# Feeding the experts' blocks: a table of tokens and a gather for each block, in place of a scatter through device memory

## The chip, the cores and the metric

One NeuronCore of a Trainium2 chip runs the whole program in one launch. Its engines are TensorE (PE; its weight loads are listed as PEld), VectorE (DVE), ScalarE (ACT), GpSimd (POOL) and SyncE (SP, which here only issues DMAs). They run their own instruction streams and meet at semaphores. The metric is the device time of the launch in microseconds; lower is better.

## The reference, cut to what matters

The reference is one step of a two-layer hybrid decoder on 512 prompt tokens and 32 sample tokens (544 rows of 1024 values, float32). Each layer ends in a mixture of experts:

```python
s = jax.nn.sigmoid((xf @ w_router).astype(f32))          # xf: (544, 1024); 16 experts in 4 groups
... e_idx: the two best experts of the best group; gates: their normalised weights, 0 elsewhere
h = jax.nn.silu(jnp.einsum('nd,edf->nef', xf, w_gate)) * jnp.einsum('nd,edf->nef', xf, w_up)
y = jnp.einsum('nef,efd->nd', h * gates[:, :, None].astype(h.dtype), w_down)   # x <- LN(alpha*x + y)
```

Every token goes to exactly two of 16 experts, so there are 1088 pairs of token and expert, 68 for an expert on average.

## The kernel before, in words

`program` gives each engine one function, and each function goes through the two layers. Everything before the experts (projections, attention, the recurrent groups, the output projection, the first norm) is left as it is by the change. Tokens lie in five tiles of `m.x`: four of 128 rows and one of 32. `MIXED_ORDER` is the order in which the first norm finishes them; `ln_done` counts them.

**Blocks.** An expert's tokens are laid in a block of 128 places. Blocks 0 to 15 belong to the experts in order; eight spare blocks (16 to 23) take what overflows 128. Their number in use is `extra_blocks`, and each engine skips them where it is 0. In the executions shown it is 0: 32 blocks are worked in two layers.

**Dispatch.** `router` (DVE, L2338) picks the experts and marks them in `m.chosen`. PE multiplies `chosen` with a triangular matrix and matrices of ones (L1184, L1186), which gives each token's place in its expert's list, into bank 6 of PSUM. `dispatch` (DVE, L2399 to L2454) turns places into row numbers `m.hi` and `m.lo`, the two slots of each token, writes them as integers to `m.slots`, and raises `idx_ready`. POOL waits for it (L586), does a one-column add (`m.turn`, L587) and a drain, and issues ten indirect DMAs (L592) that scatter the five tiles of x, twice each, into the device-memory tensor `rows_in`. This tensor was zeroed once at the start of the program.

**The block loop.** SP loads the weights of blocks 0 and 1 early (L468), waits for all ten scatters (`x_scattered`, L470), loads the rows of blocks 0 and 1 from `rows_in` (L460), and from then on, for block b, waits until the down product of block b-2 is done (L476) and issues three loads: 0.5 MB of rows, 2 MB of `w_gu`, 1 MB of `w_dn`. Two buffers of each exist. PE goes round in this order (L1227 to L1232): transposes of the rows of block b (`rows_to_columns`, L1195), transposes of the hidden values of b-1 (L1211), the down product of b-1 (L1221), the gate and up product of b (L1204). ACT copies the transposed rows and does the silu; DVE multiplies (L2468), copies the turned hidden values (L2472), and both copy results out. ACT stores each block's 0.5 MB of results to `rows_out` (L1605). DVE scales x by ALPHA for the second residual (L2464), after the scatters have read x.

**After the loop.** SP's queue goes on to the norm's and the next layer's weights as soon as block 15's are issued (L481, L483). POOL waits for the last store (L596), and ten indirect DMAs gather each token's two result rows (L602). DVE combines them, from `combine` at L2309 on, and normalises.

A semaphore's target for layer l is `nth(l, name, n)`, the total of the layers before plus n; `PER_LAYER` says how much each rises in a layer.

Of the kernel before, what the change touches and what calls it, by code (L numbers as in the profile page):

```python
# [14 lines left out]
F32 = mybir.dt.float32  # L15
# [6 lines left out]
DM = 1024  # L22
# [42 lines left out]
def counts(names):  # L65
# [8 lines left out]
    ("new_bias", 32), ("cos_q", 40), ("sin_q", 40), ("cos_i", 20), ("sin_i", 20), ("reset", TP),  # L74
    ("ones", 1), ("group_order", 4), ("expert_order", 16), ("eps", 2),
])
# [12 lines left out]
def constants():  # L89
# [45 lines left out]
    put("reset", np.broadcast_to(reset, (P, TP)))  # L135
    put("ones", np.ones((P, 1)))
    put("group_order", np.broadcast_to(4.0 - np.arange(4), (P, 4)))
    put("expert_order", np.broadcast_to(16.0 - np.arange(16), (P, 16)))
# [28 lines left out]
    router_mm=1, router_sig=1, chosen=1, slots_mm=1, idx_ready=1, x_scattered=160,  # L167
    xg0_in=8 * BLOCKS, xg1_in=8 * BLOCKS, xgt_mm=BLOCKS, xgt_copied=BLOCKS, gu_mm=BLOCKS, silu_done=BLOCKS, h_ready=BLOCKS,
    ht_mm=BLOCKS, ht_copied=BLOCKS, down_mm=BLOCKS, y_copied_a=BLOCKS, y_copied_v=BLOCKS,
# [19 lines left out]
def nth(l, name, n):  # L189

    return l * PER_LAYER[name] + (n + START.get(name, 0))
# [10 lines left out]
def memory(arena):  # L202
# [139 lines left out]
    m.beyond, m.count = view(YT0 + 656, 8, NEXP), view(YT0 + 784, 8)  # L342
    m.hi, m.lo, m.gate_hi, m.gate_lo = (view(YT0 + 792 + 5 * k, 5) for k in range(4))
    return m

def program(nc, din, dout):
    with ExitStack() as ctx:
        arena = ctx.enter_context(nc.sbuf_tensor("arena", [P, ARENA], F32))
        pages = ctx.enter_context(nc.sbuf_tensor("pages", [1, DB * NPAGE], I32))  # L350
        ints = ctx.enter_context(nc.sbuf_tensor("ints", [P, 19], I32))
        ps = ctx.enter_context(nc.psum_tensor("ps", [P, 8, 512], F32))

        s = {name: ctx.enter_context(nc.semaphore(name)) for name in (*PER_LAYER, *ONCE)}
        m = memory(arena)
        m.pages, m.slots, m.extra_expert = pages, ints[:, 0:10].rearrange("p (k i) -> p k i", k=2), ints[0:1, 10:18]
        m.extra_blocks = ints[0:1, 18:19]

        m.rows_in = nc.dram_tensor("rows_in", (BLOCKS * P, DM), F32, kind="Internal").ap()
        m.rows_out = nc.dram_tensor("rows_out", (BLOCKS * P, DM), F32, kind="Internal").ap()  # L360
        block = ctx.enter_context(nc.Block())

        @block.sync
        def _(sp):
            sync_program(sp, s, m, din, dout)

        @block.gpsimd
        def _(pool):
            pool_program(pool, s, m, din, dout)

        @block.tensor
        def _(pe):
            tensor_program(pe, s, m, ps)

        @block.scalar
        def _(act):
            scalar_program(act, s, m, ps, din, dout)

        @block.vector
        def _(dve):  # L380
            vector_program(dve, s, m, ps)
# [9 lines left out]
def sync_program(sp, s, m, din, dout):  # L391
# [16 lines left out]
    for l in range(DEPTH):  # L408
# [59 lines left out]
        for k, moe_in in enumerate((s["moe0_in"], s["moe1_in"])):  # L468
            block_weights(k, k, moe_in)
        sp.wait_ge(s["x_scattered"], nth(l, "x_scattered", 160))  # L470
        for k, xg_in in enumerate((s["xg0_in"], s["xg1_in"])):
            block_rows(k, k, xg_in)
        with sp.Fori(1, NEXP // 2) as e:
            for k, (moe_in, xg_in) in enumerate(((s["moe0_in"], s["xg0_in"]), (s["moe1_in"], s["xg1_in"]))):

                sp.wait_ge(s["down_mm"], nth(l, "down_mm", e * 2 + (k - 1)))  # L476
                block_rows(k, e * 2 + k, xg_in)
                block_weights(k, e * 2 + k, moe_in)
# [5 lines left out]
        extra = sp.value_load(m.extra_blocks, min_val=0, max_val=BLOCKS - NEXP)  # L484
        with sp.If(extra > 0):
            with sp.Fori(0, SPARE // 2) as e:
                for k, (moe_in, xg_in) in enumerate(((s["moe0_in"], s["xg0_in"]), (s["moe1_in"], s["xg1_in"]))):
                    expert = sp.value_load(m.extra_expert[0:1, bass.ds(e * 2 + k, 1)], min_val=0, max_val=NEXP - 1)
                    sp.wait_ge(s["down_mm"], nth(l, "down_mm", e * 2 + (NEXP + k - 1)))
                    block_rows(k, e * 2 + (NEXP + k), xg_in)  # L490
                    block_weights(k, expert, moe_in)

        with sp.If(extra <= 0):
            sp.wait_ge(s["down_mm"], nth(l, "down_mm", NEXP)).then_inc(s["xg0_in"], 8 * SPARE)
            sp.drain().then_inc(s["xg1_in"], 8 * SPARE)
            sp.drain().then_inc(s["moe0_in"], 16 * SPARE)
            sp.drain().then_inc(s["moe1_in"], 16 * SPARE)
# [10 lines left out]
def pool_program(pool, s, m, din, dout):  # L508
# [51 lines left out]
    for l in range(DEPTH):  # L560
# [16 lines left out]
        for g in range(2):  # L577
            with pool.Fori(0, 4) as j:
                for c in range(NPAGE):
# [3 lines left out]
                        .then_inc((s["v0_in"], s["v1_in"])[g], 16)  # L583

        pool.wait_ge(s["zeros_out"], ZEROED)
        pool.wait_ge(s["idx_ready"], nth(l, "idx_ready", 1))  # L586
# [32 lines left out]
def tensor_program(pe, s, m, ps):  # L619
# [560 lines left out]
    def experts(l):  # L1180
# [8 lines left out]

        def rows_to_columns(e, k):  # L1190

            pe.wait_ge((s["xg0_in"], s["xg1_in"])[k], nth(l, f"xg{k}_in", e * 16 + 16))
            pe.wait_ge(s["xgt_copied"], nth(l, "xgt_copied", e * 2 + k))
            for c in range(KC):
                mm = pe.transpose(ps[:, c // 4, P * (c % 4):P * (c % 4) + P], m.xg[k][:, P * c:P * c + P], ident)  # L1195
            mm.then_inc(s["xgt_mm"], 1)
# [44 lines left out]
        with pe.If(extra > 0):  # L1241
            with pe.Fori(NEXP // 2, BLOCKS // 2) as e:
                rows_to_columns(e, 0)
                gate_and_up(e, 0)
                rows_to_columns(e, 1)
                hidden_to_columns(e, 0)
# [4 lines left out]
        with pe.If(extra <= 0):  # L1251
            pe.wait_ge(s["xg0_in"], nth(l, "xg0_in", 8 * BLOCKS))
            pe.wait_ge(s["xg1_in"], nth(l, "xg1_in", 8 * BLOCKS))
            pe.wait_ge(s["moe0_in"], nth(l, "moe0_in", 16 * BLOCKS))
# [407 lines left out]
def vector_program(dve, s, m, ps):  # L1662
# [736 lines left out]
    def dispatch(l):  # L2399
# [35 lines left out]
        dve.drain()  # L2435
        tt(m.hot_lo, m.slot, m.lo.unsqueeze(2).broadcast_to([P, 5, NEXP]), ALU.is_equal)
        tt(m.hot_hi, m.hot_hi, m.gates, mul)
        ts(m.slots[:, 0, :], m.hi, -1.0, None, add)
# [14 lines left out]
        ts(m.extra_expert, m.count[0:1], float(NEXP - 1), None, ALU.min)  # L2453
        dve.drain().then_inc(s["idx_ready"], 1)  # L2454

    def experts(l):
        dve.wait_ge(s["router_sig"], nth(l, "router_sig", 1))
        router(l)
        dispatch(l)
        dve.wait_ge(s["x_scattered"], nth(l, "x_scattered", 160))  # L2460
        dve.wait_ge(s["xt_mm"], nth(l, "xt_mm", 5))
        for i in range(5):
            n = P if i < NT else NS
            ts(m.x[0:n, i, :], m.x[0:n, i, :], ALPHA, None, mul)  # L2464

        def hidden(e, k):
# [23 lines left out]
        hidden_columns(e, 1)  # L2490
        rows_back(e, 1)
        extra = dve.value_load(m.extra_blocks, min_val=0, max_val=BLOCKS - NEXP)
        with dve.If(extra > 0):
# [150 lines left out]
```

## Time and profile before

| | before |
|---|---|
| median of 3 runs | 1634.36 us (1633.82 to 1634.43) |
| the profiled execution's own time | 1633.86 us |
| its span | 1632.1 us |
| instructions | 22312 |
| PE busy / DVE / ACT / POOL | 1252.6 / 697.3 / 342.1 / 163.9 us |
| mean granted TensorE clock | 0.874 of 2.4 GHz |
| device memory traffic | 246.31 MB, mean 151 GB/s |

```text
span 1632.1 us, 22312 instructions
## 1 busy us (share of the span) xinstructions
PE 1252.6 (77%) x8296; PEld 783.5 (48%) x8296; DVE 697.3 (43%) x1425; ACT 342.1 (21%) x798; POOL 163.9 (10%) x224
## 2 busy tenths in 40 slices
PE   5989992786798188999398999819768953999960
PEld 2567772773445043444155677719434531444420
DVE  0146999545333300111353579984452451111108
ACT  0144220213322011111133422202132210111110
POOL 0120043003000200000201000700130002000001
PEclk9979996887898599999699799959979966999985
DMA  6193101005450347888711021100156103888853
GB/s 235 49 407 136 65 27 42 3 3 160 163 210 0 135 169 302 330 330 333 289 58 59 27 65 52 52 3 4 59 163 251 62 0 135 308 333 336 336 198 144
DMA packets 67918, 246.31 MB, mean 151 GB/s; under 512 B 8722, under 2 KB 29362, under 8 KB 58674
## 3 DMA queue, kind: packets, MB, share of 16 engines
q1 hardware_dynamic: 48736, 177.17, 29.5%
q0 software_dynamic: 14048, 50.00, 8.6%
q10 hardware_dynamic: 5042, 17.90, 2.7%
q8 instruction: 60, 0.98, 0.3%
q14 instruction: 32, 0.26, 0.1%
HBM read 194.39 MB, written 52.87 MB: 151 GB/s over the span
## 4 chain that ended last, share of the span: by engine, by line
PE 58%; DVE 20%; DMA 6%; issue 4%; DVEq 4%; ACT 4%; SPq 3%; POOL 1%; ACTq 0%; POOLq 0%
PE ps L1204 13%; PE ps L806 9%; PE ps L1167 7%; PE ps L1221 7%; PE ps L653 6%; PE ps L673 6%; DVE arena L2157 4%; DVE arena L2153 3%; DMA arena<-in_w_dn 2%; SPq L448 1%; PE ps L1041 1%; DMA arena<-in_wa 1%; POOL rows_in L592 1%; SPq L445 1%; DVEq L2154 1%
## 5 line engine op out<-in xcount | busy, mean ns | idle before, releaser
L1276 ACT ACTIVATE arena<-ps 128x512 f32<-128x512 f32 (+14 forms) x358 | 155.4, 470 | 792.6 <-PE ps L806 201.9
L673 PE MATMUL ps<-arena 128*128 128x272 f32 x1088 | 260.9, 399 | 0.0
L1204 PE MATMUL ps<-arena 128*128 128x512 f32 x512 | 233.1, 608 | 6.2 <-DMA arena<-in_w_dn 3.8
L673 PEld LDWEIGHTS ps<-arena 128*128 128x128 f32 x1088 | 208.7, 193 | 50.6 <-issue 5.5
L806 PE MATMUL ps<-arena 64*64 64x64 f32 (+3 forms) x4016 | 160.5, 242 | 89.4 <-DVE arena L1944 72.9
L806 PEld LDWEIGHTS ps<-arena 64*64 64x64 f32 x4016 | 145.6, 142 | 103.4 <-DVE arena L1944 73.4
L1204 PEld LDWEIGHTS ps<-arena 128*128 128x128 f32 x512 | 98.9, 194 | 135.1 <-issue 134.7
L1221 PE MATMUL ps<-arena 128*128 128x512 f32 x256 | 119.2, 609 | 19.5 <-DVE arena L2472 19.5
L653 PE MATMUL ps<-arena 128*128 128x512 f32 (+1 forms) x256 | 105.3, 572 | 22.3 <-DMA arena<-in_wa 19.1
L1167 PE MATMUL ps<-arena 128*128 128x512 f32 x256 | 114.1, 601 | 0.0
L2468 DVE TENSOR_TENSOR arena<-arena,ps 128x256 f32<-128x256 f32 x32 | 13.5, 423 | 234.3 <-ACT arena L1594 234.3
L653 PEld LDWEIGHTS ps<-arena 128*128 128x128 f32 x256 | 49.5, 196 | 74.2 <-issue 74.2
L1221 PEld LDWEIGHTS ps<-arena 128*128 128x128 f32 x256 | 46.4, 191 | 73.4 <-issue 73.4
L1195 PE MATMUL ps<-arena 128*128 128x128 f32 x256 | 35.0, 282 | 58.6 <-DMA arena<-rows_in 58.6
L2478 DVE COPY arena<-ps 128x512 f32<-128x512 f32 x32 | 22.2, 693 | 127.3 <-PE ps L1221 127.3
L1167 PEld LDWEIGHTS ps<-arena 128*128 128x128 f32 x256 | 48.1, 191 | 57.7 <-issue 57.6
L2157 DVE MATCH_REPLACE8 arena<-arena 32x544 f32<-32x544 f32 (+3 forms) x122 | 69.8, 585 | 0.6 <-issue 0.6
L2153 DVE MAX8 arena<-arena 32x8 f32<-32x544 f32 (+3 forms) x130 | 68.4, 587 | 2.2 <-issue 0.3
L1195 PEld LDWEIGHTS ps<-arena 128*128 128x128 f32 x256 | 31.1, 145 | 74.7 <-DMA arena<-rows_in 58.8
L1566 ACT ACTIVATE arena<-ps,arena 128x128 f32<-128x128 f32 (+1 forms) x120 | 41.7, 454 | 64.1 <-PE ps L1136 47.5
L1594 ACT ACTIVATE arena<-ps 128x256 f32<-128x256 f32 x32 | 12.4, 387 | 195.4 <-PE ps L1204 195.4
L1041 PE MATMUL ps<-arena 128*64 128x128 f32 x160 | 29.9, 348 | 26.8 <-ACT arena L1276 26.8
(348 smaller groups left out, 1254.4 us busy)
## 6 DMA issues: line engine op xcount, KB each, us to landing
arena<-in_w_gu SPq DMA_DIRECT2D x32, 2048.0 KB, 7.8
arena<-in_w_dn SPq DMA_DIRECT2D x32, 1024.0 KB, 10.8
arena<-in_wf SPq DMA_DIRECT2D x34, 512.0 KB, 3.8
arena<-rows_in SPq DMA_DIRECT2D x32, 512.0 KB, 3.4
rows_out<-arena ACTq DMA_DIRECT2D x32, 512.0 KB, 6.0
rows_in<-arena POOLq DMA_DIRECT2D x12, 1024.0 KB, 24.0
arena<-in_cache_v POOLq DMA_DIRECT2D x64, 128.0 KB, 2.7
arena<-in_cache_k SPq DMA_DIRECT2D x64, 128.0 KB, 2.7
```

The costliest lines, as they stand in the source:

```text
L653: mm = pe.matmul(ps[:, k % 2, 0:w], m.xT[:, c, row_tile(i)], m.wa[:, c, a:a + w], start=c == 0, stop=c == KC - 1)
L673: mm = pe.matmul(ps[:, 2 + 2 * h + n % 2, 0:HALF], m.wf[n % 3][:, c, :], m.xT[:, c, h * HALF:h * HALF + HALF], start=c == 0, stop=c == KC - 1)
L806: mm = pe.matmul(out[q], lhsT[q], rhs[q], start=start, stop=stop, skip_group_check=check)
L1041: mm = pe.matmul(ps[q, 6 + i % 2, P * (h // 2):P * (h // 2) + P], m.A[:, c, 512 + 64 * h:576 + 64 * h], m.pT[i % 2][:, h, P * c:P * c + P] ...
L1167: mm = pe.matmul(ps[:, 2 * (i % 2) + h, :], m.yT[:, c, row_tile(i)], m.wout[:, c, 512 * h:512 * h + 512], start=c == 0, stop=c == 7)
L1195: mm = pe.transpose(ps[:, c // 4, P * (c % 4):P * (c % 4) + P], m.xg[k][:, P * c:P * c + P], ident)
L1204: mm = pe.matmul(ps[:, 3, :], m.xgT[:, c, :], m.w_gu[k][:, c, :], start=c == 0, stop=c == KC - 1)
L1221: mm = pe.matmul(ps[:, 5 + h, :], m.hT[:, f, :], m.w_dn[k][:, f, 512 * h:512 * h + 512], start=f == 0, stop=f == 1)
L1276: return act.activation(out, in_, ACT.Copy)
L1566: ins = act.activation(m.xT[:, c, P * i:P * i + n], ps[:, 4 + c // 4, n * (c % 4):n * (c % 4) + n], ACT.Identity, bias=m.lnc[:, 1, c:c + 1 ...
L2153: dve.max(m.top8[c][rows], m.work[c][rows])
L2157: dve.match_replace(m.work[c][rows], m.top8[c][rows], m.work[c][rows], -3e38)
```

## The change

The rows of blocks 0 to 15 no longer come through `rows_in`. SP stores each finished tile of x to a new device-memory tensor `x_mid` (five plain DMAs, one after each `ln_done`). DVE makes two sets of one-hot matrices in `dispatch`, PE multiplies them in ten small products, and the result is a table of 128 places by 16 experts that holds the token number of each place (0 where a place is empty). DVE copies it to integers (`m.table`). POOL then issues one indirect DMA for each block, which gathers 128 rows of `x_mid` straight into `m.xg`. For block b of 2 and more it waits until b-1 down products are done, with the one-column add and a drain after each wait. SP's loop loads weights alone. The ten scatters are still issued, behind the 16 gathers in POOL's order, and only the branch for spare blocks waits for them on SP and PE; DVE waits for them, and then scales x by ALPHA, after the last block instead of before the first.

```diff
+    put("place", np.broadcast_to(np.arange(P), (P, P)))
+    put("token", P * np.arange(5)[None] + i[:, None])
...
@@ sync_program
-        sp.wait_ge(s["x_scattered"], nth(l, "x_scattered", 160))
-        for k, xg_in in enumerate((s["xg0_in"], s["xg1_in"])):
-            block_rows(k, k, xg_in)
+        for k, i in enumerate(MIXED_ORDER):
+            sp.wait_ge(s["ln_done"], nth(l, "ln_done", k + 1))
+            sp.dma_start(m.x_mid[P * i:P * i + tokens(i)], m.x[0:tokens(i), i, :]).then_inc(s["x_stored"], 16)
         with sp.Fori(1, NEXP // 2) as e:
-            for k, (moe_in, xg_in) in enumerate(((s["moe0_in"], s["xg0_in"]), (s["moe1_in"], s["xg1_in"]))):
+            for k, moe_in in enumerate((s["moe0_in"], s["moe1_in"])):
 
                 sp.wait_ge(s["down_mm"], nth(l, "down_mm", e * 2 + (k - 1)))
-                block_rows(k, e * 2 + k, xg_in)
                 block_weights(k, e * 2 + k, moe_in)
...
@@ pool_program
+        pool.wait_ge(s["x_stored"], nth(l, "x_stored", 80))
+        pool.wait_ge(s["table_ready"], nth(l, "table_ready", 1))
+        pool.tensor_tensor(m.turn, m.const("ones"), m.const("ones"), ALU.add)
+        pool.drain()
+        for b in range(NEXP):
+            if b >= 2:
+                pool.wait_ge(s["down_mm"], nth(l, "down_mm", b - 1))
+                pool.tensor_tensor(m.turn, m.const("ones"), m.const("ones"), ALU.add)
+                pool.drain()
+            pool.indirect_dma_start(m.xg[b % 2], None, m.x_mid, bass.IndirectOffsetOnAxis(ap=m.table[:, b:b + 1], axis=0))\
+                .then_inc((s["xg0_in"], s["xg1_in"])[b % 2], 16)
         pool.wait_ge(s["zeros_out"], ZEROED)
         pool.wait_ge(s["idx_ready"], nth(l, "idx_ready", 1))
...
@@ tensor_program, experts
+        pe.wait_ge(s["table_in"], nth(l, "table_in", 1))
+        for k in range(2):
+            for i in range(5):
+                n = tokens(i)
+                mm = pe.matmul(ps[:, 7, P:P + NEXP], m.here[k][0:n, i, :], m.of[k][0:n, i, :],
+                               start=k + i == 0, stop=k + i == 5)
+        mm.then_inc(s["table_mm"], 1)
...
@@ vector_program, dispatch
         tt(m.hot_lo, m.slot, m.lo.unsqueeze(2).broadcast_to([P, 5, NEXP]), ALU.is_equal)
+        tt(m.of[0], m.hot_hi, pos, mul)
+        dve.drain()
+        tt(m.of[1], m.hot_lo, pos, mul)
+        dve.tensor_reduce(m.at[0], m.of[0], AX.X, add)
+        dve.drain()
+        dve.tensor_reduce(m.at[1], m.of[1], AX.X, add)
+        token = m.const("token").unsqueeze(2).broadcast_to([P, 5, NEXP])
+        place = m.const("place").unsqueeze(1).broadcast_to([P, 5, P])
+        tt(m.of[0], m.hot_hi, token, mul)
+        tt(m.here[0], place, m.at[0].unsqueeze(2).broadcast_to([P, 5, P]), ALU.is_equal)
+        dve.drain()
+        tt(m.of[1], m.hot_lo, token, mul)
+        tt(m.here[1], place, m.at[1].unsqueeze(2).broadcast_to([P, 5, P]), ALU.is_equal)
+        dve.drain().then_inc(s["table_in"], 1)
         tt(m.hot_hi, m.hot_hi, m.gates, mul)
...
         dve.drain().then_inc(s["idx_ready"], 1)
+        dve.wait_ge(s["table_mm"], nth(l, "table_mm", 1))
+        dve.tensor_copy(m.table, ps[:, 7, P:P + NEXP])
+        dve.drain().then_inc(s["table_ready"], 1)
...
@@ vector_program, experts
         dispatch(l)
-        dve.wait_ge(s["x_scattered"], nth(l, "x_scattered", 160))
-        dve.wait_ge(s["xt_mm"], nth(l, "xt_mm", 5))
-        for i in range(5):
-            n = P if i < NT else NS
-            ts(m.x[0:n, i, :], m.x[0:n, i, :], ALPHA, None, mul)
...
         rows_back(e, 1)
+        dve.wait_ge(s["x_stored"], nth(l, "x_stored", 80))
+        dve.wait_ge(s["x_scattered"], nth(l, "x_scattered", 160))
+        for i in range(5):
+            n = P if i < NT else NS
+            ts(m.x[0:n, i, :], m.x[0:n, i, :], ALPHA, None, mul)
         extra = dve.value_load(m.extra_blocks, min_val=0, max_val=BLOCKS - NEXP)
```

## Rows read from the trace of the kernel before

**Rows 1.** The page: busy time of PE, and the chain that ended last, by engine.
```profile
PE 1252.6 (77%) x8296; PEld 783.5 (48%) x8296; DVE 697.3 (43%) x1425; ACT 342.1 (21%) x798; POOL 163.9 (10%) x224
PE 58%; DVE 20%; DMA 6%; issue 4%; DVEq 4%; ACT 4%; SPq 3%; POOL 1%; ACTq 0%; POOLq 0%
```
**Rows 2.** The chain in order of time: start us, us, what; dispatch, two blocks' products, layer 1's first transpose.
```profile
547.80 3.58 issue
562.78 3.67 DMA rows_in<-arena,ints
566.47 3.31 DMA arena<-rows_in
569.83 1.98 PE ps L1195 x8
...
645.86 6.89 PE ps L1204 x16
...
658.51 6.89 PE ps L1204 x16
...
1369.26 1.98 PE ps L1195 x8
```
**Rows 3.** Timeline, one block of layer 0: start, busy, engine, line, [idle before <-releaser].
```profile
646.02 0.35 SPq L460 DMA_DIRECT2D arena<-rows_in  x1
...
652.57 1.04 PE L1195 MATMUL ps<-arena 128*128 128x128 f32 x8
...
653.82 0.41 PE L1211 MATMUL ps<-arena 128*128 128x128 f32 x2 [0.21 <-DVE arena L2468]
```
**Rows 4.** Timeline, end of the first norm and the dispatch of layer 0.
```profile
523.92 1.23 DVE L2277 TENSOR_TENSOR arena<-arena 128x1024 f32<-128x1024 f32 x1
...
525.57 3.60 PE L1146 MATMUL ps<-arena 128*128 128x16 f32 x16 [3.06 <-ACT arena L1566]
...
545.15 0.24 DVE L2436 TENSOR_TENSOR arena<-arena 128x80 f32<-128x80 f32 x1
...
547.61 0.19 POOL L587 TENSOR_TENSOR arena<-arena 128x1 f32<-128x1 f32 x1 [131.56 <-DVEq L2454]
```
**Rows 5.** The page's DMA issues: queue, count, KB each, median us from issue to landing.
```profile
arena<-in_w_dn SPq DMA_DIRECT2D x32, 1024.0 KB, 10.8
...
rows_out<-arena ACTq DMA_DIRECT2D x32, 512.0 KB, 6.0
...
rows_in<-arena,ints POOLq DMA_INDIRECT x20, 4.1
arena<-rows_out,ints POOLq DMA_INDIRECT x20, 5.5
```
**Rows 6.** By source line: landing of ACT's 32 stores (L1605), then of the four norm loads (L404).
```profile
DMA to landing us min/median/max: 2.6/6.0/8.6
...
DMA to landing us min/median/max: 4.8/9.5/13.4
```
**Rows 7.** Timeline of POOL: what follows the one-column add, at L535 and L597.
```profile
248.35 0.19 POOL L535 TENSOR_TENSOR arena<-arena 128x1 f32<-128x1 f32 x1 [1.59 <-ACT arena L1276]
248.68 0.20 POOL L537 COPY arena<-arena 128x16 f32<-128x16 f32 x1
...
793.65 0.99 POOL L602 DMA_INDIRECT arena<-rows_out,ints  x1 [1.67 <-issue]
```
**Rows 8.** Windows of 2 us: PE, PEld, DVE, ACT, POOL, PEclk, DMA share, GB/s.
```profile
562.00:564.00 2.00, 0.00 (x0) 0.00 (x0) 0.00 (x0) 0.00 (x0) 1.33 (x2) 0.50 0.98 383
```
**Rows 9.** Timeline: the one stall of a product inside the block loop, in layer 0.
```profile
618.59 8.84 PE L1204 MATMUL ps<-arena 128*128 128x512 f32 x16 [3.12 <-DMA arena<-in_w_dn]
```
**Rows 10.** Timeline: the end of layer 0's last block, and DVE's scaling before the first block.
```profile
566.47 3.09 DVE L2464 TENSOR_SCALAR arena<-arena 128x1024 f32<-128x1024 f32 x5 [19.05 <-DMA rows_in<-arena,ints]
...
786.12 0.69 DVE L2478 COPY arena<-ps 128x512 f32<-128x512 f32 x1 [3.92 <-PE ps L1221]
...
801.53 2.66 DVE L2309 SCALAR_TENSOR_TENSOR arena<-arena 128x1024 f32<-128x1024 f32 x2 [14.72 <-DMA arena<-rows_out,ints]
```

More of the change, by code:

```diff
@@ L74 @@
     ("new_bias", 32), ("cos_q", 40), ("sin_q", 40), ("cos_i", 20), ("sin_i", 20), ("reset", TP),
-    ("ones", 1), ("group_order", 4), ("expert_order", 16), ("eps", 2),
+    ("ones", 1), ("group_order", 4), ("expert_order", 16), ("eps", 2), ("place", 128), ("token", 5),
 ])
@@ L167 @@
     router_mm=1, router_sig=1, chosen=1, slots_mm=1, idx_ready=1, x_scattered=160,
-    xg0_in=8 * BLOCKS, xg1_in=8 * BLOCKS, xgt_mm=BLOCKS, xgt_copied=BLOCKS, gu_mm=BLOCKS, silu_done=BLOCKS, h_ready=BLOCKS,
+    x_stored=80, table_in=1, table_mm=1, table_ready=1, xs0_in=8 * SPARE, xs1_in=8 * SPARE,
+    xg0_in=8 * NEXP, xg1_in=8 * NEXP, xgt_mm=BLOCKS, xgt_copied=BLOCKS, gu_mm=BLOCKS, silu_done=BLOCKS, h_ready=BLOCKS,
     ht_mm=BLOCKS, ht_copied=BLOCKS, down_mm=BLOCKS, y_copied_a=BLOCKS, y_copied_v=BLOCKS,
@@ L343, in memory @@
     m.hi, m.lo, m.gate_hi, m.gate_lo = (view(YT0 + 792 + 5 * k, 5) for k in range(4))
+    m.at = [view(YT0 + 812 + 5 * k, 5) for k in range(2)]
+    m.of = [view(YT0 + 832 + 80 * k, 5, NEXP) for k in range(2)]
+    m.here = [view(YT0 + 992 + 640 * k, 5, P) for k in range(2)]
     return m
@@ L350, in program @@
         pages = ctx.enter_context(nc.sbuf_tensor("pages", [1, DB * NPAGE], I32))
-        ints = ctx.enter_context(nc.sbuf_tensor("ints", [P, 19], I32))
+        ints = ctx.enter_context(nc.sbuf_tensor("ints", [P, 19 + NEXP], I32))
         ps = ctx.enter_context(nc.psum_tensor("ps", [P, 8, 512], F32))
@@ L357, in program @@
         m.extra_blocks = ints[0:1, 18:19]
+        m.table = ints[:, 19:19 + NEXP]
+        m.x_mid = nc.dram_tensor("x_mid", (T, DM), F32, kind="Internal").ap()
         m.rows_in = nc.dram_tensor("rows_in", (BLOCKS * P, DM), F32, kind="Internal").ap()
@@ L485, in sync_program @@
         with sp.If(extra > 0):
+            sp.wait_ge(s["x_scattered"], nth(l, "x_scattered", 160))
             with sp.Fori(0, SPARE // 2) as e:
-                for k, (moe_in, xg_in) in enumerate(((s["moe0_in"], s["xg0_in"]), (s["moe1_in"], s["xg1_in"]))):
+                for k, (moe_in, xg_in) in enumerate(((s["moe0_in"], s["xs0_in"]), (s["moe1_in"], s["xs1_in"]))):
                     expert = sp.value_load(m.extra_expert[0:1, bass.ds(e * 2 + k, 1)], min_val=0, max_val=NEXP - 1)
@@ L493, in sync_program @@
         with sp.If(extra <= 0):
-            sp.wait_ge(s["down_mm"], nth(l, "down_mm", NEXP)).then_inc(s["xg0_in"], 8 * SPARE)
-            sp.drain().then_inc(s["xg1_in"], 8 * SPARE)
+            sp.wait_ge(s["down_mm"], nth(l, "down_mm", NEXP)).then_inc(s["xs0_in"], 8 * SPARE)
+            sp.drain().then_inc(s["xs1_in"], 8 * SPARE)
             sp.drain().then_inc(s["moe0_in"], 16 * SPARE)
@@ L1188, in experts, with rows_to_columns @@
         mm.then_inc(s["slots_mm"], 1)
-        def rows_to_columns(e, k):
-            pe.wait_ge((s["xg0_in"], s["xg1_in"])[k], nth(l, f"xg{k}_in", e * 16 + 16))
+        pe.wait_ge(s["table_in"], nth(l, "table_in", 1))
[5 more added lines that the diff above has]
+        mm.then_inc(s["table_mm"], 1)
+        def rows_to_columns(e, k, spare=False):
+            if spare:
+                pe.wait_ge((s["xs0_in"], s["xs1_in"])[k], nth(l, f"xs{k}_in", e * 16 + (16 - 8 * NEXP)))
+            else:
+                pe.wait_ge((s["xg0_in"], s["xg1_in"])[k], nth(l, f"xg{k}_in", e * 16 + 16))
             pe.wait_ge(s["xgt_copied"], nth(l, "xgt_copied", e * 2 + k))
@@ L1242, in experts @@
             with pe.Fori(NEXP // 2, BLOCKS // 2) as e:
-                rows_to_columns(e, 0)
+                rows_to_columns(e, 0, True)
                 gate_and_up(e, 0)
-                rows_to_columns(e, 1)
+                rows_to_columns(e, 1, True)
                 hidden_to_columns(e, 0)
@@ L1251, in experts @@
         with pe.If(extra <= 0):
-            pe.wait_ge(s["xg0_in"], nth(l, "xg0_in", 8 * BLOCKS))
-            pe.wait_ge(s["xg1_in"], nth(l, "xg1_in", 8 * BLOCKS))
+            pe.wait_ge(s["xs0_in"], nth(l, "xs0_in", 8 * SPARE))
+            pe.wait_ge(s["xs1_in"], nth(l, "xs1_in", 8 * SPARE))
             pe.wait_ge(s["moe0_in"], nth(l, "moe0_in", 16 * BLOCKS))
```

## The prediction

> **What bounds the kernel now.** I read the page's first part and its chain, then the chain in order of time around the two expert stages, then timelines of the dispatch, of one block and of the stage's end, and last the landing times of the transfers. The page says that PE is busy 77% of the span and holds 58% of the chain [rows 1]. The chain in order of time shows two different things that the change touches. First a hole: dispatch ends at 547.6, and the first transposes of a block start at 569.83 [rows 2, 4]. The chain runs there through POOL (3.58 us before its first scatter, then ten scatters up to 562.78), the last scatter's landing (3.67) and the rows' load (3.31) [rows 2]. Second a train: from one block's gate and up product to the next it is 658.51 - 645.86 = 12.65 us [rows 2], and the reader is to see that no transfer stands in it. PE is the bound of the train, and what feeds it has slack. The train's slack is what the change spends, so I measure it first.
>
> **The slack of a block's rows.** Let D be the end of the down product of block b-2, which is the start of a gate and up product, 645.86 [rows 2]. SP reacts at 646.02, 0.17 us later, with the load of rows [rows 3]. Block b's transposes start at 652.57, and behind them PE still waits 0.21 us for DVE before L1211 [rows 3]. So rows that land at D + 6.71 cost nothing, and up to D + 6.92 next to nothing. The landing before, at about 3.3 us from issue [rows 2], used half of this.
>
> **Part 1, the hole: what goes, what comes.** Gone from the path are nine of the ten scatters, the last one's landing, and the reload from `rows_in`. The five stores to `x_mid` are new: the last tile's norm ends at 523.92 + 2 x 1.3 = about 526.5 [rows 4], and a 0.5 MB store lands in 2.6 us at the least and 8.6 at the most [rows 6], so by 535 at the latest, 12 us before anything waits. They cost nothing, their cover being the router.
> - DVE up to `table_in`. It starts behind L2436 (545.15 + 0.24) [rows 4]. Six operations on 80 columns or fewer take about 0.24 each, less where they overlap, and two comparisons on 640 columns lie between 0.24 (80 columns) and 1.23 (1024 columns) [rows 4], by length 0.80 each. With four drains that is 1.3 + 1.6 = 2.9 us: `table_in` at 548.3.
> - PE: ten products are 20 records of a 16-column product. After a pause, 16 of these took 3.60 us, 0.225 us each [rows 4]. PE has paused since the slots' product, so 4.5 us, to 552.9. Meanwhile DVE goes on with the rest of dispatch, which ends about 550.5, so it is off the path.
> - DVE's copy to integers with its wait and drain, 0.4 us: `table_ready` at 553.3. POOL's add (0.19) and the pause before its first indirect DMA: 3.58 us before the scatters, 1.67 before the gathers of the end [rows 2, 7]. I take 3.58, since it is the same place in the program: start 557.1.
> - Landing of a gather with nothing beside it: scatters 4.1, gathers of the end 5.5, both medians [rows 5]. I take 5.0: 562.1 against 569.83. The gain is 7.7 us a layer. With 1.67 and 4.1 it is 10.5, with 3.58 and 6.5 it is 6.2. About 60 of 128 places are empty and all read token 0. The nearest row is the norm's load, 1 MB written to 128 partitions from the same 8 KB: 4.8 us at the least [rows 6]; a megabyte at 383 GB/s takes 2.7 [rows 8], plus a latency near 2, so repeated reads show no price and I take nothing.
> Layer 1 has the same hole (transposes at 1369.26 [rows 2]); two layers give -15.4 us.
>
> **Part 2, the train: 14 gathers a layer behind a wait.** For b of 2 and more POOL waits for the same event as SP did. Then 0.17 to react, 0.19 for the add, a pause g, and the landing q counted from the start of the indirect DMA. Nothing else is queued behind POOL's wait except the next gathers and the scatters. Its price is in what PE waits for.
> - g: 0.14 us where POOL had been idle for only 1.59 us [rows 7], 1.67 after a long wait in front of an indirect DMA [rows 7], 3.58 in front of the first scatter. Here POOL idles some 9 us between gathers. I take 1.67, the row with the same pair of instructions; ends 0.14 and 3.58.
> - q: no row shows an indirect DMA beside the weights' stream. Before, SP's rows stood ahead of the weights in one queue. Now the weights' 3 MB are issued about 2 us before the gather, and it has to share with them. Alone or among its like it takes 4.1 to 5.5 [rows 5]. A transfer of the same 0.5 MB that does run beside the weights is ACT's store: 2.6 at the least, 6.0 in the median [rows 5, 6], so company costs it 3.4. The scatter's 4.1 plus 3.4 is 7.5; the end's gathers at 5.5 already had each other for company. I take the middle, 6.5; ends 4.1 and 8.9.
> Sum: 0.17 + 0.19 + 1.67 + 6.5 = 8.53 after D, against 6.92. Each of the 28 gathers holds PE back by 1.6 us, and the period goes from 12.65 to about 14.3 us: 28 x 1.6 = +45 us.
>
> Here a rule bears on the sum. The rows show that company costs a 0.5 MB store 3.4 us [rows 5, 6]. The Trainium skill, page DMA: Bandwidth & Descriptors, section "Queues, rings and completion order", has each DMA engine alternate packet by packet between the queues that have work. By that rule the gather would lose only its own length once more, which is the second rival below.
>
> **Part 3, edits with one answer.** SP's loop loses a load, so weights start 0.5 us earlier; they landed 10.8 us after issue [rows 5] with 12.65 to spare, so this hides. The spare branch is not entered. DVE's scaling was 3.09 us in front of the first block [rows 10], under the rows' load. Now it follows the last copy at 786.12 + 0.69, and the first combining operation waits until 801.53 [rows 10]: 14.7 us of cover, free. Its waits on `x_stored` and `x_scattered` are long fulfilled by then, if the next point holds.
>
> **Part 4, the scatters at the end of the train.** They start when block 15's gather is issued, ten at about 1.27 us (547.61 + 0.19 + 3.58 to 562.78, nine intervals) [rows 2, 4], so 12.7 us of POOL, long before the last product. But their 4.4 MB run beside block 15's 3 MB of weights. Up to D + 3.3 the weights have the engines to themselves (about 0.7 MB at 383 GB/s [rows 8]); the other 2.3 MB at half of it take 12 us: landed at about D + 15.8 against D + 14.3 needed. That is +1.5 us a layer, between 0 and 5, so +3. In layer 0 the next layer's weights then reach into the last store and the final gathers: +1.5.
>
> **Sum.** Against the profiled execution's 1633.86: -15.4 + 45 + 3 + 1.5 = +34, so 1668 us; the median of the runs is 0.5 us above that execution, so I say **1668.5**.
>
> **The rivals.**
> - *The gathers come in time.* If g is 0.14 to 0.3 as after POOL's short pause [rows 7] and q under 6.3, the sum is at most 6.9 after D and no block waits. Then only the hole counts: -15.4, with block 15's weights now late against D + 12.65 by 3.1 us a layer, and 1.5: 1634.4 - 15.4 + 6.2 + 1.5 = 1626.7. For it: POOL waits 9 us here, not 100 or more. Against it: both kinds of indirect DMA that follow the add show 1.67 or 3.58, none less. It is faster than before.
> - *The fair share.* The gather loses only its own length, 0.5 MB at 383 GB/s = 1.37 us [rows 8]: q = 4.1 + 1.4 = 5.5, and with g = 1.67 the sum is 7.5, a delay of 0.6. 28 x 0.6 = 17: 1634.4 - 15.4 + 17 + 4.5 = 1640.5. That is the time by the rule named above. Against it stands the store's 3.4. The losing side begins where a block's delay passes 0.4 us.
> - *The clock falls as well.* The one stall in the train, 3.12 us of PE, was followed by a product of 8.84 us instead of 6.89 [rows 2, 9]: the granted clock had fallen from 2.4 to 1.2 GHz. If q is near 8.5 (delay 3.6 us), each block pays 3.6 + 1.95 = 5.6 us: 28 x 5.6 = 156, so 1780. It decides from a delay of about 3 us; at 1.6 it doesn't come in. Against: it needs the upper end of q or g = 3.58 each time.
> Where the Trainium skill, page TensorE: Matmul & The Clock Gate, section "HAM oscillation — how this bites in real kernels", describes a product that starts cold after every wait for data, the trace shows it once, in that row.
> - *The change doesn't remove the hole*, because the table's ten products and the pause cost what the scatters did: it would need 7 us more than my steps. Small.
>
> **How the numbers follow.** Late gathers (delay 0.8 to 2.9 us, so 1645 to 1704): 0.48. Gathers in time: 0.24. Fair share, 0.2 to 0.8: 0.14. Clock falls: 0.11. Others: 0.03. A measurement here can tell about 0.2%, 3.3 us. The in-time case is faster by more than that. The fair-share case spans 1629 to 1645 and lies mostly above: 0.03 faster, 0.05 within, 0.06 slower. Faster 0.28, same 0.06, slower 0.66. Range: from the in-time case (1620, where the hole also gives its 10 us) to the late case's upper end and a little of the clock's, 1712. The late case's own range is 1645 to 1704.
>
> **What would show it.** In the profile after: the first transposes of a stage some 8 us earlier against the router's end; the period from one gate and up product to the next at 14.3 us, with PE's idle time before the transposes at L1195's place ended by a DMA from `x_mid`, about 1.6 us for each of 28; landing of the 32 gathers with a median near 6.5 but nearer to 5 for blocks 0 and 1; POOL's pause after each add. A period of 12.65 would prove the sum wrong at g or q. A period over 17 with a granted clock well below 1 in the stage would be the clock's case. A late product of block 15 that waits for `w_dn` would be part 4.

## The result and the profile after

The changed kernel takes **1842.3 us** (median of 4 runs, 1832.2 to 1847.0) against 1634.1 us (median of 4) for the kernel before: a ratio of 1.127, 95% interval 1.121 to 1.133. It is slower by some 208 us. The forecast was 1668.5 with a range of 1620 to 1712, so the direction was right and the size was wrong by a factor of six.

| | before | after |
|---|---|---|
| median of the runs | 1634.1 us | 1842.3 us |
| the profiled execution's time / span | 1633.86 / 1632.1 us | 1846.99 / 1845.3 us |
| PE busy | 1252.6 us | 1347.0 us |
| mean granted clock | 0.874 | 0.833 |
| `issue` in the chain that ended last | 4% | 32% |
| gather of a block, issue to landing | (rows by SP, 3.4) | 10.7 us |

The page of the kernel after, busy time and the chain by engine, answers to [rows 1]:

```profile
PE 1347.0 (73%) x8336; PEld 836.9 (45%) x8336; DVE 704.5 (38%) x1443; ACT 342.2 (19%) x798; POOL 199.8 (11%) x286
PE 36%; issue 32%; DVE 17%; DVEq 4%; DMA 3%; ACT 3%; SPq 2%; POOL 2%; POOLq 0%; ACTq 0%
```

PE is busier by 94 us although only 40 small records are new, and a third of the chain is now `issue`, time for which the profile shows no releaser. Neither says by itself where the time is. The chain in order of time does (start, length, what). It answers to [rows 2]:

```profile
560.02 3.52 issue
...
589.49 18.34 issue
609.87 18.32 issue
...
868.19 5.53 PE ps L1251 x8
873.73 6.90 PE ps L1234 x16
882.71 3.69 PE ps L1251 x8
```

The train has gone from a row of products to a row of 18 us pieces without a releaser, one for each block, 20.4 us apart instead of 12.65. The last lines show that it is over at once where it ends: the product of block 15 (873.73) has its old 6.90 us and the last down product its 3.69.

**The hole closed as forecast.** The timeline of the dispatch after (start, busy, engine, line, operation, idle before) answers to [rows 4, 7]:

```profile
551.48 0.24 DVE L2466 TENSOR_TENSOR arena<-arena 128x80 f32<-128x80 f32 x1
...
552.71 0.82 DVE L2476 TENSOR_TENSOR arena<-arena 128x640 f32<-128x640 f32 x1
...
554.66 4.78 PE L1213 MATMUL ps<-arena 128*128 128x16 f32 x20 [7.91 <-DVEq L2480]
...
559.84 0.19 POOL L595 TENSOR_TENSOR arena<-arena 128x1 f32<-128x1 f32 x1 [141.18 <-DVEq L2501]
563.55 1.03 POOL L602 DMA_INDIRECT arena<-x_mid,ints  x1 [3.52 <-issue]
564.88 0.96 POOL L602 DMA_INDIRECT arena<-x_mid,ints  x1 [0.30 <-issue]
568.18 1.97 PE L1225 MATMUL ps<-arena 128*128 128x128 f32 x8 [8.74 <-DMA arena<-x_mid,ints]
```

From the same operation (`hot_lo`, 551.48 here, 545.15 before) to the first transposes it is 16.70 us, where it was 24.68: 7.98 us less, forecast 7.7 (in layer 1 it is 16.5 us where it was 24.8). Each step is within 0.4 us of its estimate: the comparison on 640 columns 0.82 (0.80), the table's product 4.8 (4.5), the pause before the first gather 3.52 (3.58), its landing 568.18 - 563.55 = 4.6 (5.0).

**The train did not hold.** One block of the kernel after, which answers to [rows 3]:

```profile
607.87 0.20 POOL L600 TENSOR_TENSOR arena<-arena 128x1 f32<-128x1 f32 x1 [18.38 <-PE ps L1251]
...
607.98 0.35 SPq L464 DMA_DIRECT2D arena<-in_w_gu  x1
608.51 0.34 SPq L465 DMA_DIRECT2D arena<-in_w_dn  x1
608.92 0.95 POOL L602 DMA_INDIRECT arena<-x_mid,ints  x1 [0.85 <-issue]
...
619.76 1.97 PE L1225 MATMUL ps<-arena 128*128 128x128 f32 x8 [5.09 <-DMA arena<-x_mid,ints]
...
622.76 5.37 PE L1251 MATMUL ps<-arena 128*128 128x512 f32 x8 [0.61 <-DVE arena L2513]
```

POOL reacts in time and its pause is only 0.85 us. But the gather issued at 608.92 releases the transposes at 619.76, 10.8 us later. PE stands idle for 5.09 us. Then come two losses that are not the wait: the eight transposes take 1.97 us (1.04 before) and the down product 5.37 (3.67). From D = 607.79 to the transposes it is 11.97 us (6.72 before, +5.25), from there to the down product 3.00 (2.27, +0.73), and that product costs 1.70 more: +7.68 us a block, 28 times, +215. With the hole's -16 this is +199 of the 208 measured. The rest I can't place: layer 0 reaches the first block's dispatch 6.3 us later in this execution, and single runs of one kernel differ by some 20 us in the comparisons below.

The same block in windows of 2 us (PE, PEld, DVE, ACT, POOL, PEclk, DMA share, GB/s), compare [rows 8, 9]:

```profile
611.00:613.00 2.00, 2.00 (x6) 0.95 (x5) 0.00 (x0) 0.00 (x0) 0.00 (x0) 1.00 0.99 418
...
617.00:619.00 2.00, 0.00 (x0) 0.00 (x0) 0.00 (x0) 0.00 (x0) 0.00 (x0) 1.00 0.90 279
619.00:621.00 2.00, 1.24 (x6) 1.24 (x7) 0.00 (x0) 0.00 (x0) 0.00 (x0) 0.59 0.85 348
621.00:623.00 2.00, 1.39 (x7) 1.02 (x6) 0.42 (x1) 1.02 (x1) 0.00 (x0) 0.50 0.02 8
```

Two things are to be seen. The granted clock falls from 1.00 (2.4 GHz) to 0.50 (1.2 GHz) about when the gather lands, and is still there at the transposes and the down product. And the DMA engines are busy until 621, more than 1 us beyond the gather's landing. What each queue moved shows where the gather stood (packets, MB, share of the engines' time; q1 is SP's queue with the weights, q0 POOL's with the gather), from 611 to 613, from 613 to 615 and from 615 to 617 us:

```profile
q1 hardware_dynamic: 51, 0.84, 98.9%
...
q1 hardware_dynamic: 46, 0.66, 77.5%
q0 software_dynamic: 38, 0.16, 18.9%
...
q1 hardware_dynamic: 61, 0.42, 60.5%
q0 software_dynamic: 64, 0.26, 39.9%
```

Before 613, which is over 4 us after its issue, not one packet of the gather moves, and the weights have moved 1.4 of their 3.1 MB. From then on the two queues move packets side by side, about one for one: between the first and the last of the gather's 128 data packets lie 129 of the weights. But a packet of the gather holds 4 KB, and one of the weights 16 KB (`w_gu`) or 8 KB (`w_dn`), so the gather gets the smaller part of the bytes and needs 5.6 us for its 0.5 MB. The other gathers of layer 0 beside weights are like it: the first packet 4.2 to 4.4 us after issue, the last at 9.7 to 10.2. `w_dn` lands behind the gather, 12.8 us after an issue 0.4 us earlier. Landing times by source line, of the 32 gathers (L602) and then of the w_gu and w_dn loads (L464, L465), answer to [rows 5, 6]:

```profile
DMA to landing us min/median/max: 4.4/10.7/11.0
...
DMA to landing us min/median/max: 8.3/8.6/20.3
...
DMA to landing us min/median/max: 12.2/12.8/22.3
```

The 4.4 belong to the first gathers, which had no weights beside them.

### The profile page after: what moved, and what is told of

It reads as the page before. It is cut to its first block, busy times and chain, and to the rows that moved or that the text cites. A ratio compares the mean times of both kernels' runs of the same rounds, so it can differ in the third digit from the quotient of the medians.

```text
span 1845.3 us, 22436 instructions
## 1 busy us (share of the span) xinstructions
PE 1347.0 (73%) x8336; PEld 836.9 (45%) x8336; DVE 704.5 (38%) x1443; ACT 342.2 (19%) x798; POOL 199.8 (11%) x286
## 4 chain that ended last, share of the span: by engine, by line
PE 36%; issue 32%; DVE 17%; DVEq 4%; DMA 3%; ACT 3%; SPq 2%; POOL 2%; POOLq 0%; ACTq 0%
PE ps L825 8%; PE ps L1186 6%; PE ps L672 6%; PE ps L692 5%; DVE arena L2187 4%; DVE arena L2183 3%; POOL arena L602 2%; SPq L456 1%; DMA arena<-x_mid,ints 1%; PE ps L1251 1%; PE ps L1060 1%; DMA arena<-in_wa 1%; DVEq L2184 1%; SPq L453 1%; DVE arena L1837 1%
## 5 line engine op out<-in xcount | busy, mean ns | idle before, releaser
L692 PEld LDWEIGHTS ps<-arena 128*128 128x128 f32 x1088 | 209.3, 194 | 50.6 <-issue 5.5
L1234 PE MATMUL ps<-arena 128*128 128x512 f32 x512 | 229.5, 600 | 2.4 <-ACT arena L1306 2.4
L1251 PE MATMUL ps<-arena 128*128 128x512 f32 x256 | 167.3, 813 | 19.5 <-DVE arena L2513 19.5
L1225 PE MATMUL ps<-arena 128*128 128x128 f32 x256 | 60.8, 416 | 161.2 <-DMA arena<-x_mid,ints 161.2
L1234 PEld LDWEIGHTS ps<-arena 128*128 128x128 f32 x512 | 98.2, 192 | 128.0 <-issue 128.0
L1225 PEld LDWEIGHTS ps<-arena 128*128 128x128 f32 x256 | 48.8, 217 | 185.5 <-issue 156.5
L1251 PEld LDWEIGHTS ps<-arena 128*128 128x128 f32 x256 | 65.2, 269 | 107.2 <-issue 107.2
L1186 PE MATMUL ps<-arena 128*128 128x512 f32 x256 | 112.4, 594 | 0.0
L2513 DVE COPY arena<-ps 128x256 f32<-128x256 f32 x32 | 13.6, 425 | 187.9 <-PE ps L1241 187.9
L672 PEld LDWEIGHTS ps<-arena 128*128 128x128 f32 x256 | 49.6, 196 | 75.1 <-issue 75.1
L1186 PEld LDWEIGHTS ps<-arena 128*128 128x128 f32 x256 | 47.4, 189 | 56.7 <-issue 56.6
L600 POOL TENSOR_TENSOR arena<-arena 128x1 f32<-128x1 f32 x28 | 5.4, 194 | 523.6 <-PE ps L1251 523.6
## 6 DMA issues: line engine op xcount, KB each, us to landing
arena<-in_w_dn SPq DMA_DIRECT2D x32, 1024.0 KB, 12.8
```

Of the source, the lines that this page charges most:

```text
L672: mm = pe.matmul(ps[:, k % 2, 0:w], m.xT[:, c, row_tile(i)], m.wa[:, c, a:a + w], start=c == 0, stop=c == KC - 1)
L692: mm = pe.matmul(ps[:, 2 + 2 * h + n % 2, 0:HALF], m.wf[n % 3][:, c, :], m.xT[:, c, h * HALF:h * HALF + HALF], start=c == 0, stop=c == KC - 1)
L1186: mm = pe.matmul(ps[:, 2 * (i % 2) + h, :], m.yT[:, c, row_tile(i)], m.wout[:, c, 512 * h:512 * h + 512], start=c == 0, stop=c == 7)
L1234: mm = pe.matmul(ps[:, 3, :], m.xgT[:, c, :], m.w_gu[k][:, c, :], start=c == 0, stop=c == KC - 1)
L1251: mm = pe.matmul(ps[:, 5 + h, :], m.hT[:, f, :], m.w_dn[k][:, f, 512 * h:512 * h + 512], start=f == 0, stop=f == 1)
```

## The experiments

Three questions were open: whether the gather's lateness is the whole loss, what of the loss is the clock, and what makes a 4.6 us gather take 10.7. Seven kernels were run; all are edits of the changed kernel; comparisons are with the kernel before on the same chip (medians 1636.5 and 1638.4 there).

**1. The same gather, asked for earlier.** A gather may overwrite `m.xg` as soon as the transposes of block b-2 have read it.

```diff
-                pool.wait_ge(s["down_mm"], nth(l, "down_mm", b - 1))
+                pool.wait_ge(s["xgt_mm"], nth(l, "xgt_mm", b - 1))
```

> One wait of the changed kernel is moved: for block b POOL waits until the transposes of block b-2 have read the buffer, not until that block's down product is done. That event lies about 18 us before the down product's end in the changed kernel and about 18 us (12.65 + 5.9) before the block's own transposes at a period of 12.65. Theory A (the gather is slow only beside the weights, lands some 11 us after issue, and its lateness is the whole loss): the gather is hidden, the period falls from 20.4 to 12.65 us, the granted clock of the stage stays at 1.0, and only the earlier start of the stage is left: 1634 - 2 x 8 = about 1618 us. Theory B (gathers through the software queue cost the stage bandwidth, so that the weights are late): the period stays over 14 us and the time over 1660, with the gate and up product waiting for w_dn.

Measured: 1632.1 us (1622.3 to 1642.8, 10 runs), ratio to the kernel before 0.997 (0.994 to 1.000). The gathers' landing, by source line:

```profile
DMA to landing us min/median/max: 4.1/5.3/6.7
```

The chain of layer 1's train:

```profile
1375.13 3.67 PE ps L1251 x8
1378.80 6.89 PE ps L1234 x16
1387.78 3.69 PE ps L1251 x8
1392.17 12.50 DMA arena<-in_w_dn
1404.80 7.16 PE ps L1234 x16
...
1547.07 15.72 DMA arena<-in_w_dn
1562.83 10.12 PE ps L1234 x16
```

One moved wait takes back 210 us: the loss is the 28 late gathers and what they cause. Theory A's period of 12.65 is there again (1375.13 to 1387.78), and the stage's clock is back. The gather is now issued when the last block's weights have almost run out, and most of it moves before the next block's are issued. But theory A's time of 1618 is missed by 14 us: weights are late in places. The product of block 15 waits for `w_dn`, which lands 15.7 us after its issue, and then runs at the lower clock. Which transfers delay it is tested in 5.

**2. PE kept busy while it waits.** Five products of 512 columns ahead of the wait, into an unused bank.

```diff
+            for c in range(fill):
+                pe.matmul(ps[:, 4, :], m.xgT[:, c, :], m.w_gu[1 - k][:, c, :], start=c == 0, stop=c == fill - 1)
             if spare:
...
-                rows_to_columns(e + k, 1 - k)
+                rows_to_columns(e + k, 1 - k, fill=5)
```

> The changed kernel with five extra 512-column products (10 records, 4.3 us) ahead of the wait for blocks 1 to 15's rows; their result goes to an unused bank and is not read. They fit into the 5.0 to 5.4 us in which PE stands idle. If the loss of a block is 5.1 us of waiting plus a fallen clock (transposes 1.97 instead of 1.03 us, down product 5.4 instead of 3.67), the granted clock in the stage goes to 1.0, the period from 20.4 to about 17.9 us and the time from 1842 to about 1842 - 28 x 2.5 = 1772. If the transposes and down products are long for another reason, the time stays at 1842 or rises.

Measured: 1771.6 us (2 runs), forecast 1772. The timeline of one block:

```profile
625.71 0.94 POOL L602 DMA_INDIRECT arena<-x_mid,ints  x1 [0.85 <-issue]
631.31 4.46 PE L1220 MATMUL ps<-arena 128*128 128x512 f32 x10
...
636.55 1.09 PE L1227 MATMUL ps<-arena 128*128 128x128 f32 x8 [0.78 <-DMA arena<-x_mid,ints]
...
638.46 3.67 PE L1253 MATMUL ps<-arena 128*128 128x512 f32 x8 [0.61 <-DVE arena L2515]
```

The gather takes as long as ever (625.71 to 636.55), PE does useless work in the meantime, and the transposes and the down product have their old lengths. So about 70 of the 208 us are the fallen clock and not the wait itself: with PE busy in the wait the clock stays up. The period is 17.6 us. This is a measurement and no remedy: the wait is still there.

**3. The gather issued ahead of the weights.** SP waits for a semaphore that POOL raises behind each gather (SP's loop is written out, which changes nothing else).

```diff
+            pool.tensor_tensor(m.turn, m.const("ones"), m.const("ones"), ALU.add).then_inc(s["gathered"], 1)
+            pool.drain()
...
                 sp.wait_ge(s["down_mm"], nth(l, "down_mm", e * 2 + (k - 1)))
+                sp.wait_ge(s["gathered"], nth(l, "gathered", e * 2 + (k + 1)))
```

> The changed kernel, but SP issues a block's weights only after POOL has issued that block's gather (a semaphore raised by an add right behind it), some 2.2 us later than now. If the gather is slow because it stands behind the weights' bytes already in the engines' queues, it lands in 5 to 6 us after issue, the block's transposes start about 7.5 us after the down product, the weights land at about 2.2 + 13 us, and the period is about 15.5 us: 1842 - 28 x 4.9 = about 1705. If its share while in flight is what is small, it still lands about 10 us after issue, and the period stays near 20 us (1842 or a little more).

Measured: 1678.1 us (2 runs), less than either theory gave. Two blocks:

```profile
586.72 0.94 POOL L603 DMA_INDIRECT arena<-x_mid,ints  x1 [0.78 <-issue]
...
587.96 0.35 SPq L464 DMA_DIRECT2D arena<-in_w_gu  x1
588.35 0.43 SPq L465 DMA_DIRECT2D arena<-in_w_dn  x1
592.38 1.03 PE L1228 MATMUL ps<-arena 128*128 128x128 f32 x8
...
600.77 8.79 PE L1237 MATMUL ps<-arena 128*128 128x512 f32 x16 [2.45 <-DMA arena<-in_w_dn]
```

The gather's landing, over all 32 by its line (least, median, most), and what each queue moved from 588 to 590 us:

```profile
DMA to landing us min/median/max: 4.3/4.7/5.4
...
q0 software_dynamic: 102, 0.41, 76.1%
q1 hardware_dynamic: 2, 0.03, 6.6%
```

The weights' loads are issued 1.24 us behind the gather, but 0.41 of its 0.52 MB have moved by 590, when only two packets of the weights have started; its first packet comes 1.64 us after issue and not 4.3. With the order turned round it lands in time and the transposes start 6.7 us after the down product, as before the change. Of my two theories the first (weights issued ahead of it) gave the landing, and I had still priced it too high. But the gather of the changed kernel doesn't stand behind all of them: its queue record above shows a late start behind about half of the weights, and then packets side by side with the rest. The weights pay for it: 16 of the 28 products wait for `w_dn`, 35.5 us in all; the one shown waits 2.45 us and then takes 8.79 us instead of 6.89.

**4. Fewer bytes of weights, and other rows.** Two runs on what the landing depends on.

```diff
-                block_weights(k, e * 2 + k, moe_in)
+                sp.dma_start(m.w_gu[k], layer_of(din["w_gu"], l * NEXP + (e * 2 + k))).then_inc(moe_in, 16)
+                sp.dma_start(m.w_dn[k][:, :, 0:128], layer_of(din["w_dn"], l * NEXP + (e * 2 + k))[:, :, 0:128]).then_inc(moe_in, 16)
```

> The changed kernel, with the loads of w_dn for blocks 2 to 15 cut to 128 of 1024 columns (the rest of the down weights is stale, so results of these blocks are wrong): 2.1 MB beside a gather instead of 3.1 MB. If the gather lands only when the stream of weights runs dry, its landing falls from 10.7 us by about the 2.3 us that the missing 0.9 MB take, to 8.4, and each block is 2.3 us shorter: 1842 - 28 x 2.5 = about 1772. If it gets a fixed share of the engines from the start, it lands as before at 10.7 us, and the time stays at 1842.

Measured: 1744.3 us (2 runs). The landing of the gathers, by their line:

```profile
DMA to landing us min/median/max: 4.3/8.5/9.8
```

8.4 us was the number of the first theory, and the second (a fixed share of the engines from the start) is out. The number does not prove the first: the gather's first packet comes 4.2 to 4.5 us after issue as before, so nothing ahead of it got shorter. What got shorter is the part side by side, some 3.5 us where it was 5.6, with 0.7 MB of weights in it where it was 1.4. The edit also cuts the packets of `w_dn` from 8 KB to 512 bytes; what fewer bytes and what smaller packets do was not told apart. The time fell by 98 instead of 70 us, since a shorter wait (2.92 us) leaves the transposes at full clock (1.09 us) and costs only the down product (5.30).

```diff
         dve.tensor_copy(m.table, ps[:, 7, P:P + NEXP])
+        dve.drain()
+        dve.tensor_copy(m.table.rearrange("p (a b) -> p a b", b=4), m.const("token")[:, 0:4].unsqueeze(1).broadcast_to([P, 4, 4]))
```

> The changed kernel with the table overwritten by four columns of distinct, ascending token numbers (so every block works on wrong rows): no row is read twice in a gather, where now some 60 of 128 places read token 0. If the repeated row is what makes a gather slow beside the weights, its landing falls from 10.7 toward 6 us and the time by up to 28 x 5 = 140 us. If only the company of the weights counts, both stay: 10.7 us and 1842.

Measured: 1840.3 us (2 runs); the landing is 10.5 us in the median, and PE waits 154.3 us for gathers where it was 161.2. The 60 empty places that all read token 0 cost nothing that matters.

**5. The scatters.** First they are left out of the changed kernel:

```diff
...
-                pool.indirect_dma_start(m.rows_in, bass.IndirectOffsetOnAxis(ap=m.slots[0:n, k, i:i + 1], axis=0),
-                                        m.x[0:n, i, :], None).then_inc(s["x_scattered"], 16)
+        pool.drain().then_inc(s["x_scattered"], 160)
```

> The changed kernel without its ten scatters (left out of the computation; no spare block needs them here). In it the scatters start only when block 15's gather has landed, and no product waits for w_dn. If the loss is in the 28 waits for gathers alone, the time stays within 5 us of 1842. If the scatters hold up the end, it falls by 10 us or more.

Measured: 1839.6 us (2 runs), no difference that the noise lets one see (runs of the changed kernel lie between 1832 and 1847). Then in the kernel of experiment 1 they are put behind a branch, so that spare blocks still work:

```diff
+        extra = pool.value_load(m.extra_blocks, min_val=0, max_val=BLOCKS - NEXP)
+        with pool.If(extra > 0):
...
+        with pool.If(extra <= 0):
+            pool.drain().then_inc(s["x_scattered"], 160)
```

> The kernel with the early wait, and the ten scatters issued only in a branch of POOL that is entered where spare blocks are in use (they are not in these inputs). With the early wait alone the time was 1632 against 1636.5 of the kernel before; its trace shows block 15's product waiting for w_dn (2.5 us and a fallen clock in layer 0; the loads landed 15.7 us after issue in layer 1, where the train lost some 8 us against before). Theory A (the scatters' 4.4 MB beside block 15's weights did that): w_dn of block 15 lands in about 11 us, layer 0 gains about 5 and layer 1 about 8 us: about 1619. Theory B (the train is late for the gathers beside the weights in every block): the end stays slow, and the time stays at 1630 or more.

Measured: **1621.7 us** (1616.5 to 1624.4, 9 runs), ratio to the kernel before 0.990 (0.987 to 0.994), against 0.997 with the scatters. The end of layer 1's train:

```profile
1547.59 3.67 PE ps L1255 x8
1551.26 6.89 PE ps L1238 x16
1560.25 3.69 PE ps L1255 x8
```

Block 15 doesn't wait any more: the scatters were what delayed its `w_dn`. This version beats both kernels, by 1.0% and 12%. What is left against the 1618 of my first expectation are small waits for `w_dn` in mid-train (five, 3.6 us in all, with products of 7.16 us behind them). Likely they come from the gathers, which move on the same engines, but the kernel before has such a wait too (0.68 us at 747.77), and this was not tested.

## Why the prediction was wrong in size

**The hole (part 1): right.** -7.98 us (layer 0) against -7.7, each step within 0.4 us.

**The pause g (part 2): too high.** Taken 1.67, measured 0.85; it hid 0.8 us of the error in q.

**The landing q (part 2): the step that failed.** I took q = 6.5 us, between ends of 4.1 and 8.9, and it is 10.7. The sum had one term for the weights' company, at most 3.4 us on top of the 5.5 of a gather of the stage's end. That the rows' load goes from before the weights to behind them in the order of issue had no term. The runs show two costs, and together they are more than I allowed. The gather's first packet moves 4.3 us after issue behind the weights and 1.64 ahead of them (experiment 3), which is 2.7 us. And 0.5 MB that goes packet for packet with 16 KB and 8 KB packets takes 5.6 us, where it is 2.2 to 2.8 us in experiment 3. ACT's store was a poor yardstick: it is issued some 6 us behind the weights, when about two thirds of them have moved. It starts late too (its first packet comes 3.3 to 4.2 us after issue beside the weights of layer 0 of the changed kernel). The row of `w_dn` itself, landing 10.8 us after issue [rows 5], would have given the right number, partly by luck: the gather lands before `w_dn` and not behind it. Why a transfer that is issued just behind the weights starts 2.7 us late was not tested.

**The forecast's rival of the clock: right as a mechanism, given 0.11.** I let it come in from a delay of about 3 us and put its price at 1.95 us a block on the gate and up product. With q = 10.7 and g = 0.85 my own sum gives a delay of 0.17 + 0.19 + 0.85 + 10.7 - 6.92 = 5.0 us, and 28 x (5.0 + 1.95) - 15.4 = +179. The measured wait is 5.09. The clock's share is larger, 2.4 us and not 1.95, since transposes and down product come first after the wait and both ran at 1.2 GHz. Experiment 2 gives that share alone: about 70 us. The row that I took the price from is not the only stall of the kernel before: a second, of 0.68 us, has a product of 7.14 us behind it, so a short one cost no clock.

**The fair share: the price was wrong, the rule is not.** I had taken from the Trainium skill (DMA: Bandwidth & Descriptors, "Queues, rings and completion order"), by which the engines alternate between queues packet by packet, that the gather would lose only its own length and land in 5.5 us. It landed in 10.7. The trace agrees with the rule once both queues have packets in flight: 128 data packets of the gather beside 129 of the weights. What doesn't follow from it is an equal share of the bytes, since the weights' packets are two to four times as long: the gather lost 1.3 to 1.5 MB of weights to them and not 0.5. The 2.7 us of late start come on top, and this rule gives no reason for them.

**The scatters (part 4): right, but hardly here.** In the changed kernel no product waits for them, and leaving them out changed the time by no more than the noise (experiment 5: 1839.6 us). They do reach into the end of layer 0: from DVE's last copy to the first combining operation it is 17.5 us, where it was 14.7 before the change and is 13.1 without scatters. I had allowed 1.5 us for this and it is 2.8. Where the train runs at 12.65 us, w_dn of block 15 landed 15.7 us after its issue, my estimate being about 15, and the scatters cost 0.7% of the time, about 11 us, where I had 6.2 plus 1.5.

**Edits with one answer (part 3): right.** DVE waits 2.50 us for the scatters before it scales x in layer 0, but the scaling lies under the last store, and nothing waits for it.

## What to carry to other kernels

When a load is taken out of a queue where it stood ahead of a big stream and is issued from another queue behind that stream, cost it as landing near the stream's end, not as a transfer of its own size: look up when its first packet moves, and count the packets it alternates with by their size. Ask of each wait which event really frees the buffer: here the transposes' semaphore instead of the down product's, one line, was worth 210 us. And where PE comes to wait, count the products behind the wait at the lower clock too: waits of 2.9 and of 5.1 us both brought it down here, and the longer one cost 2.4 us on top of itself.

## What the runs showed that I had not expected

- An issue order that differs by 2.2 us (1.24 ahead of the first weights' load, or 0.94 behind it) decides between 4.7 and 10.7 us of landing.
- The granted clock still read 1.00 in the first windows of the idle stretch and fell at its end: a wait of 2.92 us left the transposes at full speed (1.09 us) and slowed the down product behind them (5.30).
- POOL's first scatter behind a gather did not start, in these traces, until about the time that gather had landed, though no semaphore asks for it. In the changed kernel it waited 10.47 us after the one-column add at 855.36, in the kernel of experiment 1 4.76 us; back to back, indirect DMAs of one kind are 0.30 us apart. What it waits for was not tried.

```profile
855.36 0.20 POOL L606 TENSOR_TENSOR arena<-arena 128x1 f32<-128x1 f32 x1
...
866.02 1.00 POOL L611 DMA_INDIRECT rows_in<-arena,ints  x1 [10.47 <-issue]
```
